# First half of the FFN's plain up tile multiplied inside the output projection stage, in accumulators that both stages share

## The chip, the core and the metric

The kernel runs on one core of one Trainium2 chip. The metric is the device time of one execution in microseconds; the kernel before has a median of 2820.73 us over three runs (2819.88 to 2821.73).

## The reference

An encoder of two layers over x (1024 tokens x 1024 features, float32). Layer 0 mixes tokens by differential attention, layer 1 by 2-D neighbourhood attention; each is followed by an output projection, a layer norm, a gated ConvFFN and another layer norm:

```python
x = layer_norm(alpha * x + mix, ln_g[i, 0], ln_b[i, 0])      # mix = heads @ w_o (+ b_o in layer 1)
ff = conv_ffn(x, ffn_w_in[i], ...)                             # h = x @ w_in + b_in; width-3 conv over tokens;
                                                               # u, g = split(h); (u * gelu(g)) @ w_out + b_out
x = layer_norm(alpha * x + ff, ln_g[i, 1], ln_b[i, 1])
```

`w_in` is 1024 x 5632: 22 tiles of 128 columns for u and 22 for g.

## The kernel before

All tensors are float32. A product is made of three matmuls in a rounded float32 form: each operand is split into a high part (a copy to the rounded form) and a low part (full minus high), and high x high, high x low and low x high are summed in PSUM.

The program is a row of stages, each with its own block of five instruction streams: attention, `output_stage` (L974), `ffn_stage` (L1155), and the same for layer 1. Between two blocks stands a barrier of all engines (`Mem.clear`, L40), and each block's buffers and PSUM are given back there. SBUF tiles X (the tokens by 128), XTh and XTl (X transposed, high and low), WH and WL (weights, eight row tiles) and `raw` (two full-precision weight slots) live across stages.

**Output stage.** Eight tiles of 128 tokens. TensorE forms `heads @ w_o` for a tile in a PSUM buffer of 1024 columns (`pg` 0 and 1 for tiles 4 to 7 in turn). VectorE adds alpha * X (`add`, L1127), in layer 1 also the bias (L1136, for tiles 4 to 7; GpSimd does it for tiles 0 to 3), takes the statistics (L913 to L917) and multiplies by the gain (L924). GpSimd takes the root of the variance (L941). Then either ScalarE scales (L948) and GpSimd shifts (L953), or, for the tiles in FINISHED (6 and 7), VectorE does both in `finish` (L932). TensorE transposes the tile (`turn`, L960, eight 128x128 transposes into `tp` 0 or 1 in turn), ScalarE makes XTh of it (`high`, L965) and VectorE XTl (`low`, L970). The turns that follow the last products (TURNS[7]) are those of tiles 5, 6 and 7; a turn waits until the low part two tiles before is done, since that frees its buffer. Both of the FFN's first two weight tiles (u tile 0 and g tile 0) are prefetched into `raw` during this stage, and at its end, behind the root of tile 7 and once all products are done, GpSimd rounds and splits them into WH[:, 6:8] and WL[:, 6:8] (L1058, L1060).

**FFN stage.** Column tile 0 (PLAIN = 1 tile) is multiplied plainly: `up_plain(a, half)` (L1408) for a = 0 (u) and 1 (g), 24 matmuls of 512 tokens for each half. The other 21 tiles go by Strassen-like sums of quarter blocks: `up_seven(f)` makes seven products M5, M2, M1, M3, M4, M7, M6 of 12 matmuls each (L1447). Their weights come in four pieces per tile (SyncE, L1286); GpSimd adds them (L1351), ScalarE makes the high part (L1614), GpSimd the low part (L1358). Their moving sides are five mixes of X: VectorE adds or subtracts token blocks (`mix_tokens`, L1794), TensorE turns them (`turn_mix`, L1423), ScalarE and VectorE split them (L1594, L1710); the fifth comes from matmuls with an identity (`sum_mix`, L1436). Small parameter vectors come as rows (L1273 to L1275) and are turned by five transposes (L1547), which wait for the three DMAs; ScalarE copies them out (L1638).

The order on TensorE before: up_plain(0, 0), the parameter transposes, turn_mix(B1), up_plain(0, 1), turn_mix(B3), up_plain(1, 0), turn_mix(B4), up_plain(1, 1), turn_mix(B7), then `up_seven(1)`: M5, M2, sum_mix(B6), M1, M3, M4, M7, M6, and `up_seven(2)`. M5 of tile 1 writes the second half of PSUM buffer 0 and M2 the first half of buffer 1, so they wait until ScalarE has taken the plain u tile (`take(0)`) and g tile (`take(1)`, L1572 and L1575). ScalarE rescales X by alpha once all four token mixes are made (L1645, L1652), before the takes. GpSimd's sum for slot i waits for product i - 4 (`made`). SyncE's queue is in order: pieces of tile 1, the bias b_out, down(0), down(1), which waits until all of X has got its bias (L1340, L1788), pieces of tile 2.

Of the kernel before, what the change touches and what calls it, by code (L numbers as in the profile page):

```python
# [20 lines left out]
P = 128  # L21
# [949 lines left out]
                                     op=ALU.subtract).then_inc(self.low_done, 1)  # L971


def output_stage(nc, name, OT, w_o, b_o, x, g, b, X, XTh, XTl, ident, alpha, raw, wh, wl, next_tiles):  # L974

# [4 lines left out]
    with ExitStack() as ctx:  # L982
# [1 line left out]
        prefetch = Prefetch(m, raw, next_tiles)  # L984
        oraw = m.sb("oraw", [P, 2, S])
        bias = m.sb("bias", [P, D])
        pg = [m.ps(f"pg{i}", [P, D]) for i in range(2)]
        tp = [m.ps(f"tp{i}", [P, KT, P]) for i in range(2)]
        FIRST = 4
        sums = [pg[0][:], pg[1][:], tp[0][:].rearrange("p k n -> p (k n)"), tp[1][:].rearrange("p k n -> p (k n)")]  # L990
# [6 lines left out]
        bias_in = m.sem("bias_in")  # L997
        first_low = m.sem("first_low")
        w_high, w_low, o_high, o_low = m.sem("w_high"), m.sem("w_low"), m.sem("o_high"), m.sem("o_low")
        product, summed, with_bias = (m.sem(s) for s in ("product", "summed", "with_bias"))  # L1000
        block = ctx.enter_context(nc.Block())

# [27 lines left out]
        @block.gpsimd  # L1030
        def _(pool):
            norm.set_power(pool)
            for k in range(1, KT):
                pool.wait_ge(w_high, k + 1)
                nc.gpsimd.tensor_tensor(out=wl[:, k], in0=raw[:, k % 2], in1=wh[:, k].bitcast(F32),
                                        op=ALU.subtract).then_inc(w_low, 1)

            def biased(t):

                pool.wait_ge(summed, t + 1)  # L1040
                nc.gpsimd.tensor_tensor(out=X[:, t], in0=X[:, t], in1=bias[:], op=ALU.add).then_inc(with_bias, 1)

            if b_o is not None:
                pool.wait_ge(bias_in, 16)
                for t in range(FIRST - 1):
                    biased(t)
            pool.wait_ge(norm.gb_in, 32)
            for t in range(TT):
                norm.root(pool, t)
                if b_o is not None and t == 0:  # L1050
                    biased(FIRST - 1)
                if t not in FINISHED:
                    norm.shift(pool, t)
            pool.wait_ge(product, TT)
            prefetch.wait(pool)
            for k in range(2):
                at = KT - 2 + k
                nc.gpsimd.tensor_scalar(wh[:, at], raw[:, k], 1.0, 1.0, ALU.mult, ALU.mult).then_inc(w_high, 1)  # L1058
                pool.wait_ge(w_high, KT + k + 1)
                nc.gpsimd.tensor_tensor(out=wl[:, at], in0=raw[:, k], in1=wh[:, at].bitcast(F32),  # L1060
                                        op=ALU.subtract).then_inc(w_low, 1)

        @block.tensor
        def _(pe):
            def products(t, k):
                for n, (o, w) in enumerate(((XTh, wh), (XTh, wl), (XTl, wh))):
                    for half in range(D // BANK):
                        last = nc.tensor.matmul(sums[t][:, half * BANK:(half + 1) * BANK],
                                                o[:, k, t * P:(t + 1) * P], w[:, k, half * BANK:(half + 1) * BANK],
                                                start=(k == 0 and n == 0), stop=(k == KT - 1 and n == 2))  # L1070
                if k == KT - 1:
                    last.then_inc(product, 1)

            for k in range(KT):
                if k == 0:
                    pe.wait_ge(first_low, 1)
                else:
                    pe.wait_ge(w_low, k)
                if k >= READY_HEADS:
                    pe.wait_ge(o_low, k - READY_HEADS + 1)  # L1080
                for t in range(FIRST):
                    products(t, k)
            for t in range(FIRST, TT):
                pe.wait_ge(summed, t - FIRST + 1 if t < FIRST + 2 else t - 1)
                for k in range(KT):
                    products(t, k)
                for u in TURNS[t]:
                    if u < 2:
                        pe.wait_ge(summed, u + 3)
                    norm.turn(pe, u)  # L1090

        @block.scalar
        def _(act):
            if b_o is not None:
                act.dma_start(bias[:], b_o.rearrange("(o d) -> o d", o=1).to_broadcast([P, D])).then_inc(bias_in, 16)
            for k in range(KT):
                if k >= 2:
                    act.wait_ge(w_in[k % 2], 16 * (k // 2))
                nc.scalar.activation(wh[:, k], raw[:, k % 2], ACT.Copy).then_inc(w_high, 1)
                if k < READY_HEADS:  # L1100
                    continue
# [12 lines left out]
        @block.vector
# [38 lines left out]


def ffn_stage(nc, name, w_in_d, b_in, conv_w, conv_b, w_out, b_out, g, b, x_out, X, XTh, XTl, ident, alpha, last_layer,  # L1155
              wraw, WH, WL, WHf, next_tiles):

# [19 lines left out]
    with ExitStack() as ctx:  # L1179
# [13 lines left out]
        prow = WDf[0:NT, 0, 0:5 * P].rearrange("p (c n) -> p c n", c=5)  # L1193
        bias = WDf[:, 1]
        gain_rows = WHf[:, 4:6]
        ph = [m.ps(f"ph{i}", [P, KT, P]) for i in range(2)]
        po = m.ps("po", [P, 4, BANK])
        flat = [ph[i][:].rearrange("p k n -> p (k n)") for i in range(2)]
        P11, P12, P21, P22 = (flat[i][:, h * BANK:(h + 1) * BANK] for i in range(2) for h in range(2))
        U = po[:, 3]  # L1200
        FINISHED = (TT - 1,)
# [197 lines left out]

        @block.tensor  # L1400
        def _(pe):
            def up_plain(a, half):
                if a and half == 0:
                    pe.wait_ge(par_set, 1)
                at = slice(half * BANK, (half + 1) * BANK)
                for k in range(KT):
                    for n, (w, x) in enumerate(((WH, XTh), (WH, XTl), (WL, XTh))):
                        last = nc.tensor.matmul(flat[a][:, at], w[:, 6 + a, k * P:(k + 1) * P], x[:, k, at],  # L1408
                                                start=(k == 0 and n == 0), stop=(k == KT - 1 and n == 2))
                if half:  # L1410
                    last.then_inc(up_done, 1)

            def turn_mix(c):

# [126 lines left out]
                            for u in range(TT - 4, TT):  # L1541
                                norm.turn(pe, u)

            up_plain(0, 0)
            pe.wait_ge(par_in, 48)
            for c in range(5):
                last = nc.tensor.transpose(flat[1][:, c * NT:(c + 1) * NT], prow[:, c], ident[0:NT, 0:NT])  # L1547
            last.then_inc(par_turned, 1)
            turn_mix(B1)
            up_plain(0, 1)  # L1550
            turn_mix(B3)
            up_plain(1, 0)
            turn_mix(B4)
            up_plain(1, 1)
            turn_mix(B7)
            for f in range(PLAIN, FT):
                up_seven(f)
# [5 lines left out]
        def _(act):  # L1563
# [71 lines left out]
            quad_copy(PLAIN, M5)  # L1635
            quad_copy(PLAIN, M2)
            act.wait_ge(par_turned, 1)
            nc.scalar.activation(par[:].rearrange("p c n -> p (c n)"), flat[1][:, 0:5 * NT], ACT.Copy).then_inc(par_set, 1)  # L1638
            mix_copy(B1)
            quad_copy(PLAIN, M1)  # L1640
            quad_copy(PLAIN, M3)
# [777 lines left out]
def build(nc, x, attn_w_qkv, attn_w_o, attn_lambda, attn_subln_g, na_w_qkv, na_b_qkv, na_rpb, na_w_o, na_b_o,  # L2419
# [10 lines left out]
    with ExitStack() as ctx:  # L2430
# [9 lines left out]
        for i in range(depth):  # L2440
            if i == 1:
                neighbourhood_stage(nc, na_w_qkv[0], na_b_qkv[0], Z, OT, XTh, XTl, ident, S, GW, KROWS, KCOLS, raw,
                                    first_rows[1])
            with ExitStack() as layer:
                X = layer.enter_context(nc.sbuf_tensor(f"X{i}", [P, S // P, D], F32))
                WH = layer.enter_context(nc.sbuf_tensor(f"WH{i}", [P, D // P, D], F32R))
                WHf = nc.alloc_sbuf_tensor_at(f"WHf{i}", [P, D // P, D], F32, offset=nc.sbuf_base - 4 * D // P * D)
                WL = layer.enter_context(nc.sbuf_tensor(f"WL{i}", [P, D // P, D], F32R))
                output_stage(nc, f"wo{i}", OT, (attn_w_o, na_w_o)[i][0], (None, na_b_o[0])[i], (x_dram, x1)[i],
                             ln_g[i, 0], ln_b[i, 0], X, XTh, XTl, ident, alpha, raw, WH, WL, first_up[i])  # L2450
                ffn_stage(nc, f"ff{i}", ffn_w_in[i], ffn_b_in[i], ffn_conv_w[i], ffn_conv_b[i], ffn_w_out[i], ffn_b_out[i],
                          ln_g[i, 1], ln_b[i, 1], (x1, out_dram)[i], X, XTh, XTl, ident, alpha, i == depth - 1, raw, WH,
                          WL, WHf, first_qk)


_INS = ["x", "attn_w_qkv", "attn_w_o", "attn_lambda", "attn_subln_g", "na_w_qkv", "na_b_qkv", "na_rpb", "na_w_o",
# [18 lines left out]
```

## Time and profile before

| | us |
|---|---|
| median of 3 runs | 2820.73 |
| the profiled execution | 2821.15 |
| its span | 2819.2 |
| TensorE busy in the span | 2661.5 (94%) |
| VectorE busy | 1937.4 (69%) |
| GpSimd busy | 1675.8 (59%) |
| ScalarE busy | 1183.6 (42%) |

The mean granted TensorE clock is 0.976 of full speed. Layer 0's output stage ends and its FFN stage begins at 773 us of the span, layer 1's at 2122.8 us. In the profile PE is TensorE, DVE VectorE, ACT ScalarE, POOL GpSimd, SP SyncE. Matmuls overlap, so a group's busy time is longer than the distance of their starts. A row of a timeline has the start and the length in us, the engine, the line, the operation, output and inputs, the count, and in brackets the engine's idle time before it with what ended it. A row of the chain has start, length and count. A row of busy time has the stretch, its length, the busy us of PE, its weight loads, DVE, ACT and POOL, the granted TensorE clock (1.00 is 2.4 GHz, its other level is 1.2), the DMA share and GB/s.

### The profile page before, as it was taken

Reading aid. Unit: us, or ns where it says so; the run is one execution under the profiler, and the core shown is the slowest. Engines: PE = TensorE matmul, PEld = TensorE weight load, DVE = VectorE, ACT = ScalarE, POOL = GpSimd, SP = SyncE. Lnnn points to the kernel's source line nnn. Section 1 sums busy time; section 2 is a strip of 40 time slices with the busy share of each in tenths; the row PEclk is TensorE's granted clock in tenths of the full one; section 3 lists DMA queues with packets and bytes.
Section 4 is the critical chain, followed back from the end, with each engine's and each line's share of the span. In section 5 each row is a group of like instructions: output and inputs, shape, how many; then the busy total and the mean of one; then the engine's idle time right before and its main releaser. Section 6 shows DMA issues by size and latency. Waiting matters only on the chain. (4 is left out here: it accounts for less than half of the span.)

```text
span 2819.2 us, 35798 instructions
## 1 busy us (share of the span) xinstructions
PE 2661.5 (94%) x13043; PEld 2224.7 (79%) x13043; DVE 1937.4 (69%) x2476; ACT 1183.6 (42%) x1762; POOL 1675.8 (59%) x1179
## 2 busy tenths in 40 slices
PE   7999999988899999999989999998798999999997
PEld 6888888776778888888867888887677888888886
DVE  3666676683677766677783777777567777666778
ACT  3455445553253333333333555555415333333332
POOL 2434443334487767777754666664457776677776
PEclk9999999998999999999999999999899999999999
DMA  3010000235021112121221221212411111121212
GB/s 116 26 30 30 28 22 30 61 96 176 11 65 48 45 57 64 46 60 46 65 85 44 60 59 45 52 44 53 134 61 54 58 47 45 60 60 45 60 45 90
DMA packets 214043, 163.82 MB, mean 58 GB/s; under 512 B 36283, under 2 KB 195595, under 8 KB 213899
## 3 DMA queue, kind: packets, MB, share of 16 engines
q1 hardware_dynamic: 213755, 161.38, 19.4%
q8 instruction: 89, 1.46, 0.2%
q14 instruction: 55, 0.45, 0.1%
q10 hardware_dynamic: 144, 0.52, 0.1%
HBM read 137.24 MB, written 24.64 MB: 57 GB/s over the span
## 5 line engine op out<-in xcount | busy, mean ns | idle before, releaser
L1351 POOL TENSOR_TENSOR ff_Rlf<-raw_weights 128x512 f32<-128x512 f32 x210 | 330.8, 1588 | 53.4 <-PE ff_ph L1447 33.1
L1358 POOL TENSOR_TENSOR ff_Rl<-ff_Rlf,ff_Rh 128x512 fp32r<-128x512 f32 x210 | 310.8, 1497 | 25.1 <-ACT ff_Rh L1614 25.1
L1358 POOL TENSOR_TENSOR ff_Rl<-raw_weights,ff_Rh 128x512 fp32r<-128x512 f32 x84 | 157.9, 1889 | 253.5 <-ACT ff_Rh L1614 253.5
L1614 ACT ACTIVATE ff_Rh<-ff_Rlf 128x512 fp32r<-128x512 f32 x210 | 130.5, 630 | 364.1 <-POOL ff_Rlf L1351 363.8
L1447 PE MATMUL ff_ph<-XTh,ff_Rh 128*128 128x512 f32 x672 | 263.0, 391 | 8.1 <-POOL ff_Rl L1358 7.8
L1447 PE MATMUL ff_ph<-XTl,ff_Rh 128*128 128x512 f32 x672 | 262.3, 390 | 0.0
L1447 PE MATMUL ff_ph<-XTh,ff_Rl 128*128 128x512 f32 x672 | 262.3, 390 | 0.0
L1494 PE MATMUL ff_po<-ff_WDh,WH 128*128 128x512 f32 x624 | 244.6, 392 | 1.8 <-DVE X L1861 1.8
L1494 PE MATMUL ff_po<-ff_WDh,WL 128*128 128x512 f32 x624 | 242.9, 389 | 0.0
L1494 PE MATMUL ff_po<-ff_WDl,WH 128*128 128x512 f32 x624 | 242.9, 389 | 0.0
L1717 DVE TENSOR_TENSOR X<-ff_po,X 128x512 f32<-128x512 f32 x288 | 191.3, 683 | 66.0 <-PE ff_po L1494 66.0
L2058 POOL TENSOR_SCALAR na_E<-na_E,na_rden 128x512 f32<-128x512 f32 x128 | 104.6, 818 | 194.0 <-DVE na_rden L2405 193.3
L687 ACT ACTIVATE da_E<-da_S,da_mn 128x1024 f32<-128x1024 f32 x112 | 125.1, 1117 | 198.0 <-DVE da_mn L782 197.8
L1725 DVE SCALAR_TENSOR_TENSOR ff_C<-ff_H,ff_par,ff_C 128x1024 f32<-128x1024 f32 x88 | 161.8, 1838 | 53.9 <-ACT ff_C L1631 52.5
L1447 PE MATMUL ff_ph<-WH,ff_Rl 128*128 128x512 f32 x504 | 196.1, 389 | 0.0
L1447 PE MATMUL ff_ph<-WL,ff_Rh 128*128 128x512 f32 x504 | 196.1, 389 | 0.0
L1447 PE MATMUL ff_ph<-WH,ff_Rh 128*128 128x512 f32 x504 | 196.1, 389 | 0.0
L324 POOL TENSOR_SCALAR da_E<-da_E,da_rden,da_neglam 128x1024 f32<-128x1024 f32 x64 | 76.6, 1197 | 198.5 <-DVE da_rden L790 198.5
L1731 DVE SCALAR_TENSOR_TENSOR ff_C<-ff_H,ff_par,ff_C 128x1024 f32<-128x1024 f32 x88 | 166.1, 1887 | 1.0
L782 DVE CUSTOM_DVE_ANT_0 da_S<-da_S,da_strip 128x1024 f32<-128x1024 f32 x128 | 154.0, 1241 | 12.1 <-PE da_S L418 11.8
L404 PE MATMUL da_pa<-XTh,da_wh 128*128 128x512 f32 x360 | 151.0, 419 | 10.0 <-POOL da_wl L318 3.8
L1447 PEld LDWEIGHTS ff_ph<-XTh,ff_Rh 128*128 128x128 f32 x672 | 126.5, 188 | 38.1 <-issue 10.8
(319 smaller groups left out, 7466.5 us busy)
## 6 DMA issues: line engine op xcount, KB each, us to landing
raw_weights<-in_ffn_w_in SPq DMA_DIRECT2D x168, 256.0 KB, 3.4
ff_WDlf<-in_ffn_w_out SPq DMA_DIRECT2D x40, 512.0 KB, 4.3
raw_weights<-in_attn_w_qkv SPq DMA_DIRECT2D x24, 512.0 KB, 3.7
raw_weights<-in_na_w_qkv SPq DMA_DIRECT2D x24, 512.0 KB, 4.2
rpb_rows<-da_rows SPq DMA_DIRECT2D x2, 3840.0 KB, 26.8
na_B<-rpb_rows SPq DMA_DIRECT2D x32, 224.0 KB, 4.5
wo_oraw<-heads_t SPq DMA_DIRECT2D x12, 512.0 KB, 4.6
da_E<-in_x SPq DMA_DIRECT2D x8, 512.0 KB, 6.2
```

The lines of the kernel that those rows point to most:

```text
L404: last = nc.tensor.matmul(out[:], w[:, j // 2, k], x[:, k, t0:t0 + BANK], start=(i == 0), stop=(i == 3 * KT - 1))
L687: nc.scalar.activation(E[:, t % 2, c], Sc[c][:], ACT.Exp, scale=-1.0, bias=mn[:, t % 2, c:c + 1], accum_out=den[:, t % 2, c:c + 1]).then_i ...
L782: nc.vector.tensor_tensor_reduce(out=Sc[c][:], in0=Sc[c][:], in1=strip[:, (QT - 1 - t) * P:(QT - 1 - t) * P + S], scale=1.0, scalar=3.0e38 ...
L1351: nc.gpsimd.tensor_tensor(out=Rf[:, i % SLOTS], in0=quad(*a), in1=quad(*b), op=op).then_inc(quad_sum, 1)
L1358: nc.gpsimd.tensor_tensor(out=Rl[:, i % SLOTS], in0=src, in1=Rh[:, i % SLOTS].bitcast(F32), op=ALU.subtract).then_inc(quad_low, 1)
L1447: last = nc.tensor.matmul(out, w, x[:, k], start=(k == 0 and n == 0), stop=(k == HK - 1 and n == 2))
L1494: last = nc.tensor.matmul(out, a[:, t * P:(t + 1) * P], w[:, half * BANK:(half + 1) * BANK], start=(f == first and j == 0), stop=(f == las ...
L1614: nc.scalar.activation(Rh[:, i % SLOTS], src, ACT.Copy).then_inc(quad_high, 1)
L1717: nc.vector.tensor_tensor(out=at, in0=po[:, r % 4], in1=at, op=ALU.add).then_inc(added, 1)
L1725: nc.vector.scalar_tensor_tensor(out=C[:, parity], in0=H[:, parity, 0:S], scalar=par[:, 1, idx:idx + 1], in1=C[:, parity], op0=ALU.mult, o ...
L1731: nc.vector.scalar_tensor_tensor(out=C[:, parity], in0=H[:, parity, 2:S + 2], scalar=par[:, 3, idx:idx + 1], in1=C[:, parity], op0=ALU.mul ...
L2058: nc.gpsimd.tensor_scalar(E[:, b], E[:, b], rden[:, b:b + 1], 1.0, ALU.mult, ALU.mult).then_inc(scaled, 1)
```

## The change

In both layers the two PSUM buffers of 1024 columns are allocated outside the stages (`acc`), and serve as `pg` in the output stage and as `ph` in the FFN stage. The first half (tokens 0 to 511) of both plain up tiles is multiplied in the output stage, `up_half(0)` between the turns of tiles 6 and 7, `up_half(1)` behind the turn of tile 7. For that, GpSimd rounds and splits the prefetched weights into buffers of their own (`up_high`, `up_low`) behind the root of tile 6, and not behind that of tile 7; WH[:, 6:8] and WL[:, 6:8] are still in use by the last products then. ScalarE copies the high part to WH and GpSimd the low part to WL when all products are done. In the FFN stage `up_plain` does the second half alone, and the five parameter transposes use the other half of their buffer.

```diff
@@ output_stage
+        up_high, up_low = m.sb("up_high", [P, 2, D], F32R), m.sb("up_low", [P, 2, D], F32R)
-        pg = [m.ps(f"pg{i}", [P, D]) for i in range(2)]
+        pg = acc
...
@@ output_stage, gpsimd
+            def split_up():
+                prefetch.wait(pool)
+                for k in range(2):
+                    nc.gpsimd.tensor_scalar(up_high[:, k], raw[:, k], 1.0, 1.0, ALU.mult, ALU.mult).then_inc(up_rounded, 1)
+                    pool.wait_ge(up_rounded, k + 1)
+                    nc.gpsimd.tensor_tensor(out=up_low[:, k], in0=raw[:, k], in1=up_high[:, k].bitcast(F32),
+                                            op=ALU.subtract).then_inc(up_split, 1)
...
                 if t not in FINISHED:
                     norm.shift(pool, t)
+                if t == TT - 2:
+                    split_up()
             pool.wait_ge(product, TT)
-            prefetch.wait(pool)
+            pool.wait_ge(up_split, 2)
             for k in range(2):
-                at = KT - 2 + k
-                nc.gpsimd.tensor_scalar(wh[:, at], raw[:, k], 1.0, 1.0, ALU.mult, ALU.mult).then_inc(w_high, 1)
-                pool.wait_ge(w_high, KT + k + 1)
-                nc.gpsimd.tensor_tensor(out=wl[:, at], in0=raw[:, k], in1=wh[:, at].bitcast(F32),
-                                        op=ALU.subtract).then_inc(w_low, 1)
+                nc.gpsimd.tensor_scalar(wl[:, KT - 2 + k], up_low[:, k].bitcast(F32), 1.0, 1.0, ALU.mult,
+                                        ALU.mult).then_inc(up_copied, 1)
@@ output_stage, tensor
+            def up_half(a):
+                pe.wait_ge(up_split, a + 1)
+                pe.wait_ge(summed, TT - 1 + a)
+                for k in range(KT):
+                    for n, (w, x) in enumerate(((up_high, XTh), (up_high, XTl), (up_low, XTh))):
+                        nc.tensor.matmul(acc[a][:, 0:BANK], w[:, a, k * P:(k + 1) * P], x[:, k, 0:BANK],
+                                         start=(k == 0 and n == 0), stop=(k == KT - 1 and n == 2))
...
                     if u < 2:
                         pe.wait_ge(summed, u + 3)
+                    if u == TT - 1:
+                        pe.wait_ge(norm.low_done, TT // 2)
+                        up_half(0)
                     norm.turn(pe, u)
+            up_half(1)
@@ output_stage, scalar
                 for u in TURNS[t]:
+                    if u == TT - 1:
+                        act.wait_ge(product, TT)
+                        act.wait_ge(up_rounded, 2)
+                        for k in range(2):
+                            nc.scalar.activation(wh[:, KT - 2 + k], up_high[:, k].bitcast(F32), ACT.Copy).then_inc(up_copied, 1)
                     norm.high(act, u)
@@ ffn_stage
-        ph = [m.ps(f"ph{i}", [P, KT, P]) for i in range(2)]
+        ph = [a[:].rearrange("p (k n) -> p k n", n=P) for a in acc]
@@ ffn_stage, tensor
-            def up_plain(a, half):
-                if a and half == 0:
+            def up_plain(a):
+                at = slice(BANK, 2 * BANK)
+                if a:
                     pe.wait_ge(par_set, 1)
-                at = slice(half * BANK, (half + 1) * BANK)
...
-                if half:
-                    last.then_inc(up_done, 1)
+                last.then_inc(up_done, 1)
...
-            up_plain(0, 0)
             pe.wait_ge(par_in, 48)
             for c in range(5):
-                last = nc.tensor.transpose(flat[1][:, c * NT:(c + 1) * NT], prow[:, c], ident[0:NT, 0:NT])
+                last = nc.tensor.transpose(flat[1][:, BANK + c * NT:BANK + (c + 1) * NT], prow[:, c], ident[0:NT, 0:NT])
             last.then_inc(par_turned, 1)
             turn_mix(B1)
-            up_plain(0, 1)
+            up_plain(0)
             turn_mix(B3)
-            up_plain(1, 0)
+            up_plain(1)
             turn_mix(B4)
-            up_plain(1, 1)
             turn_mix(B7)
@@ build
+                acc = [layer.enter_context(nc.psum_tensor(f"acc{i}_{j}", [P, D], F32)) for j in range(2)]
```

## Rows read from the trace of the kernel before

**Rows 1.** Waits of TensorE, layer 0's FFN stage: total us, times, longest us.

```profile
PE ff_ph L1447 <- POOL ff_Rl L1358: 3.1, 1, 3.1
```

**Rows 2.** Timeline, layer 0's FFN head: start us, us, engine, line, tiles [idle before].

```profile
780.69 2.52 POOL L1351 TENSOR_TENSOR ff_Rlf<-raw_weights 128x512 f32<-128x512 f32 x2 [7.58 <-DMA raw_weights<-in_ffn_w_in]
...
783.24 0.63 ACT L1614 ACTIVATE ff_Rh<-ff_Rlf 128x512 fp32r<-128x512 f32 x1 [0.61 <-POOL ff_Rlf L1351]
...
793.71 3.90 ACT L1645 ACTIVATE X<-X 128x1024 f32<-128x1024 f32 x4 [2.65 <-DVE ff_WDhf L1794]
...
798.56 2.36 DVE L1710 TENSOR_TENSOR WL<-ff_po,WH 128x1024 fp32r<-128x1024 f32 x2 [2.08 <-ACT WH L1594]
...
806.21 1.22 ACT L1575 ACTIVATE ff_C<-ff_ph,ff_centre,ff_par 128x1024 f32<-128x1024 f32 x1
...
807.48 0.50 PE L1447 MATMUL ff_ph<-XTh,ff_Rh 128*128 128x512 f32 x1
...
816.59 3.53 POOL L1351 TENSOR_TENSOR ff_Rlf<-raw_weights 128x512 f32<-128x512 f32 x2
...
830.88 0.56 PE L1447 MATMUL ff_ph<-XTh,ff_Rh 128*128 128x512 f32 x1 [3.11 <-POOL ff_Rl L1358]
...
838.05 0.39 PE L1447 MATMUL ff_ph<-WH,ff_Rh 128*128 128x512 f32 x1
```

**Rows 3.** Timeline, ScalarE, head of layer 1's FFN stage.

```profile
2147.02 1.94 ACT L1594 ACTIVATE WH<-ff_po 128x1024 fp32r<-128x1024 f32 x2 [0.85 <-PE ff_po L1423]
```

**Rows 4.** Timeline, TensorE, from layer 0's output stage into the FFN stage.

```profile
759.51 1.91 PE L960 MATMUL wo_tp<-ident,X 128*128 128x128 f32 x16
...
767.66 1.94 PE L960 MATMUL wo_tp<-ident,X 128*128 128x128 f32 x8 [6.24 <-DVE XTl L970]
...
773.02 0.76 PE L1408 MATMUL ff_ph<-XTh,WH 128*128 128x512 f32 x1 [3.42 <-PEq L43]
```

**Rows 5.** Timeline, GpSimd and VectorE, end of layer 0's output stage.

```profile
764.26 1.04 POOL L1058 TENSOR_SCALAR WH<-raw_weights 128x1024 fp32r<-128x1024 f32 x1
...
764.38 1.99 DVE L932 SCALAR_TENSOR_TENSOR X<-X,wo_rstd,wo_gb 128x1024 f32<-128x1024 f32 x1 [0.51 <-POOL wo_rstd L941]
...
765.39 3.20 POOL L1060 TENSOR_TENSOR WL<-raw_weights,WH 128x1024 fp32r<-128x1024 f32 x1
...
769.69 2.35 POOL L1060 TENSOR_TENSOR WL<-raw_weights,WH 128x1024 fp32r<-128x1024 f32 x1
```

**Rows 6.** Chain that ended last, up halves of layer 1.

```profile
2122.78 8.26 PE ff_ph L1408 x24
...
2133.38 5.50 PE ff_ph L1408 x24
```

**Rows 7.** Timeline, TensorE, start of the kernel.

```profile
4.51 3.65 PE L552 MATMUL da_S<-ident,da_E 128*128 128x128 f32 x16 [4.51 <-DMA da_E<-in_x]
...
8.92 1.07 PE L552 MATMUL da_S<-ident,da_E 128*128 128x128 f32 x8 [0.76 <-DVE XTl L719]
...
34.18 0.50 PE L404 MATMUL da_pa<-XTh,da_wh 128*128 128x512 f32 x1 [2.63 <-DVE XTl L719]
```

**Rows 8.** Timeline, GpSimd and VectorE, layer 0's FFN stage at 811.

```profile
811.00 3.41 POOL L1365 TENSOR_TENSOR ff_WDl<-ff_WDlf,ff_WDh 128x1024 fp32r<-128x1024 f32 x1
...
812.05 5.66 DVE L1788 TENSOR_TENSOR X<-X,ff_WDlf 128x1024 f32<-128x1024 f32 x2
```

**Rows 9.** Timeline, end of layer 1's output stage.

```profile
2102.25 1.55 POOL L941 TENSOR_TENSOR wo_rstd<-wo_ve,wo_power 128x1 f32<-128x1 f32 x1
...
2108.02 1.91 PE L960 MATMUL wo_tp<-ident,X 128*128 128x128 f32 x16
...
2109.47 1.22 DVE L1136 TENSOR_TENSOR X<-X,wo_bias 128x1024 f32<-128x1024 f32 x1
...
2117.43 1.94 PE L960 MATMUL wo_tp<-ident,X 128*128 128x128 f32 x8 [7.50 <-DVE XTl L970]
```

**Rows 10.** Busy time of each engine by stretch, layer 0's first up half.

```profile
773.00:780.30 7.30, 7.28 (x24) 5.61 (x24) 4.49 (x2) 1.57 (x2) 0.11 (x2) 0.76 0.54 161
```

More of the change, by code:

```diff
@@ L971, in low, with output_stage @@
                                      op=ALU.subtract).then_inc(self.low_done, 1)
-def output_stage(nc, name, OT, w_o, b_o, x, g, b, X, XTh, XTl, ident, alpha, raw, wh, wl, next_tiles):
+def output_stage(nc, name, OT, w_o, b_o, x, g, b, X, XTh, XTl, ident, alpha, raw, wh, wl, next_tiles, acc):
     S, D = x.shape
@@ L999, in output_stage @@
         w_high, w_low, o_high, o_low = m.sem("w_high"), m.sem("w_low"), m.sem("o_high"), m.sem("o_low")
+        up_rounded, up_split, up_copied = m.sem("up_rounded"), m.sem("up_split"), m.sem("up_copied")
         product, summed, with_bias = (m.sem(s) for s in ("product", "summed", "with_bias"))
@@ L1155, in ffn_stage @@
 def ffn_stage(nc, name, w_in_d, b_in, conv_w, conv_b, w_out, b_out, g, b, x_out, X, XTh, XTl, ident, alpha, last_layer,
-              wraw, WH, WL, WHf, next_tiles):
+              wraw, WH, WL, WHf, next_tiles, acc):
     D = w_in_d.shape[0]
@@ L1195, in ffn_stage @@
         gain_rows = WHf[:, 4:6]
-        ph = [m.ps(f"ph{i}", [P, KT, P]) for i in range(2)]
+        ph = [a[:].rearrange("p (k n) -> p k n", n=P) for a in acc]
         po = m.ps("po", [P, 4, BANK])
-        flat = [ph[i][:].rearrange("p k n -> p (k n)") for i in range(2)]
+        flat = [a[:] for a in acc]
         P11, P12, P21, P22 = (flat[i][:, h * BANK:(h + 1) * BANK] for i in range(2) for h in range(2))
@@ L1637, in _ @@
             act.wait_ge(par_turned, 1)
-            nc.scalar.activation(par[:].rearrange("p c n -> p (c n)"), flat[1][:, 0:5 * NT], ACT.Copy).then_inc(par_set, 1)
+            nc.scalar.activation(par[:].rearrange("p c n -> p (c n)"), flat[1][:, BANK:BANK + 5 * NT], ACT.Copy).then_inc(par_set, 1)
             mix_copy(B1)
@@ L2448, in build @@
                 WL = layer.enter_context(nc.sbuf_tensor(f"WL{i}", [P, D // P, D], F32R))
+                acc = [layer.enter_context(nc.psum_tensor(f"acc{i}_{j}", [P, D], F32)) for j in range(2)]
                 output_stage(nc, f"wo{i}", OT, (attn_w_o, na_w_o)[i][0], (None, na_b_o[0])[i], (x_dram, x1)[i],
-                             ln_g[i, 0], ln_b[i, 0], X, XTh, XTl, ident, alpha, raw, WH, WL, first_up[i])
+                             ln_g[i, 0], ln_b[i, 0], X, XTh, XTl, ident, alpha, raw, WH, WL, first_up[i], acc)
                 ffn_stage(nc, f"ff{i}", ffn_w_in[i], ffn_b_in[i], ffn_conv_w[i], ffn_conv_b[i], ffn_w_out[i], ffn_b_out[i],
                           ln_g[i, 1], ln_b[i, 1], (x1, out_dram)[i], X, XTh, XTl, ident, alpha, i == depth - 1, raw, WH,
-                          WL, WHf, first_qk)
+                          WL, WHf, first_qk, acc)
 _INS = ["x", "attn_w_qkv", "attn_w_o", "attn_lambda", "attn_subln_g", "na_w_qkv", "na_b_qkv", "na_rpb", "na_w_o",
```

## The prediction

> **What bounds the kernel now.** I read the page's busy line first (TensorE 94% of the span), then who TensorE waits for in each FFN stage, then the timelines of all engines around the two changes of stage, since this edit touches only those. In layer 0's FFN stage TensorE's only long idle time besides the change of stage is 3.1 us [rows 1]. It stands at the second tile's first product, at 830.88 [rows 2]; behind it TensorE runs without a gap to the layer's end. So what counts is when that product starts, in both layers.
>
> What sets that start is in the rows between 773 and 831 [rows 2]. GpSimd forms its first weight sum at 780.69, when the pieces land that were asked for at the stage's start (7.6 us of idle). ScalarE's copy of the second sum (783.24) waits for GpSimd. The token mixes, VectorE's, follow, and at 793.71 ScalarE starts rescaling X right behind a wait for the last mix on VectorE. From there ScalarE has copies and biases without a gap to 806.21 + 1.22 = 807.43, and product M2 starts at 807.48, since it overwrites what that last ScalarE instruction (`take(1)`) reads. None of these waits names TensorE. TensorE's plain up halves lie beside this chain, and the chain hangs on the start of the stage (T0), because the weight pieces are asked for there. In layer 1 the two run level: one ScalarE copy at 2147.02 waited 0.85 us for TensorE [rows 3]. So removing up-matmuls behind T0 is worth nothing in layer 0 and at most 0.85 us in layer 1, and whatever moves T0 later is lost in full.
>
> **The end of the output stage, layer 0.** Today: TensorE turns tokens tiles 5 and 6 (759.51 + 1.91 = 761.42), idles 6.24 us, turns tile 7 at 767.66, and the FFN's first matmul is at 773.02 [rows 4]. The last to end is GpSimd's second low part, 769.69 + 2.35 = 772.04 [rows 5], so the barrier costs 0.98 us.
> After: the first up half (24 matmuls) goes into the 6.24 us. At the full clock 24 of them take 5.50 us, at the slow one, partly, 8.26 [rows 6]. TensorE comes to it from dense work, so 5.50: 761.42 to 766.9. It needs only tiles 0 to 3 and GpSimd's first split, done at about 757; free. The turn of tile 7 starts at 767.66 as before, because its release (VectorE, behind its layer norm of tile 7) doesn't move. It then takes 1.07 us and not 1.94: after an idle time of 0.76 us eight transposes took 1.07 [rows 7]. That is 768.7. Now the second half follows, 5.50, to 774.2, and TensorE is last into the barrier where GpSimd was. T0 = 774.2 + 0.98 = 775.2: **2.2 us later**. GpSimd's work there shrinks (two 1.04 us copies instead of 1.04 + 3.20 + 1.04 + 2.35), and ScalarE's two new copies fall into its own idle time: nothing. The DMA queue of SyncE has nothing moved past it before T0.
>
> **The end of the output stage, layer 1.** Here the split, moved ahead of the root of tile 7, meets a bias add that layer 0 doesn't have. Two instructions that each read two SBUF operands exclude one another on VectorE and GpSimd: two VectorE adds (1.22 each alone) took 5.66 us while GpSimd's subtraction (811.00, 3.41) and the next one ran [rows 8]; the first waited until 814.41. The same shows in rows 5: VectorE's 764.38 took 1.99, until GpSimd's 764.26 was through, and GpSimd's 765.39 took 3.20 against 2.35 alone. Now place the split: GpSimd's root of tile 6 ends at 2102.25 + 1.55 = 2103.80 [rows 9]. From there the same pattern as from 764.26 in layer 0 (rounding at 0, subtraction at +1.13 held up by VectorE's norm of tile 6, rounding at +4.30, subtraction at 769.69 - 764.26 = +5.43) puts the second subtraction at 2109.23 to 2111.58. VectorE's bias add of tile 7 wants to start at 2109.47, 0.24 us too late: it waits until 2111.58, **2.1 us**. Behind it on VectorE stand statistics, gain, finish and the low parts that free the buffer for the turn of tile 7; they all shift, and the turn starts at 2117.43 + 2.1 = 2119.5. The bounds of this wait are 0.7 (VectorE comes first, and only its gain waits) and 2.4 (a whole subtraction).
> TensorE: tiles 5 and 6 end at 2108.02 + 1.91 = 2109.93, first half to 2115.4, idle 4.1 us. After 2.63 us of idle a matmul still ran at the full clock [rows 7], after 3.11 us not: the 24 matmuls from 830.88 to 838.05 took 7.17 us, not 5.50 [rows 2]. So the turn is at the slow clock, 1.94, to 2121.45. At the kernel's start transposes alone ran slow for 3.65 us, and eight that followed were at the full clock [rows 7]; 1.7 us of slow matmuls remain, which costs half of it, 0.8. Second half: 2121.45 + 5.50 + 0.8 = 2127.75, + 0.98 = 2128.7, against 2122.78 [rows 6]: **5.9 us later**. (Bounds: turn and half at the full clock, 4.2; a half of 8.26, 7.9; without the bias wait and warm, 2.2.)
> Rows 7 bear on a rule of the Trainium skill, "TensorE: Matmul & The Clock Gate", Part 4: PE-mode transpose, by which transposes do not bring the full clock. The trace speaks against it. By the page, the second half would take 8.26 in layer 1, 2.0 us more than my 6.3.
>
> **Inside the FFN stage.** Of TensorE's work 24 matmuls of 7.28 us (granted clock 0.76 [rows 10]; 8.26 in layer 1) and 24 of 5.50 are gone. The parameter columns are then turned as soon as their DMAs land, some 4 us behind T0, where TensorE starts slow, but the first ScalarE copy that needs the first mix comes at T0 + 11 anyhow. From T0 to M2 nothing gets shorter in layer 0. M5 now starts when the last mix can be turned, behind VectorE's split of the one before it (798.56 + 2.36, T0 + 27.9 [rows 2]), at about T0 + 28.8, is through at 31.6 and M2 still has to wait for `take(1)` at T0 + 34.4. That is 2.8 us of idle, between the 2.63 that kept the clock and the 3.11 that lost it; with TensorE thinly used ahead of it I take it as lost. M2 and what follows come 1.7 to 2.8 us later (7.17 or 8.26 against 5.50), take 2.0. Most is free, as TensorE idled 3.1 us ahead of 830.88. GpSimd's sum for M6 waits for M1's end: it started at 816.59 + 1.77 = 818.36, some 1.6 behind M1, so it loses 0.4, and so do the next pieces and M5 of the next tile. But the idle time ahead of that M5 shrinks to 1.5 us, and its slow start (7.17 - 5.50 = 1.7) goes. Layer 0: 0.4 - 1.7 = **-1.3**. In layer 1 the 24 matmuls there ran at the full clock already; the late M1 costs **+0.4** and eats the 0.85. (If the clock holds through the 2.8 us: 0 in layer 0, -0.85 to +0.85 in layer 1.) The down-projection weight, asked for 2 us earlier behind T0, is the one DMA that moves; ScalarE takes it at T0 + 36: nothing. The bank that the five parameter transposes use is another one, at no cost.
>
> **Sum.** 2.2 + 5.9 - 1.3 + 0.4 = 7.2 us. The profiled execution took 2821.15 us (span 2819.2, so 2 us around it), 0.4 above the median 2820.73: 2821.15 + 7.2 - 0.4 = 2828.0, 0.26% slower.
>
> **Rivals.**
> No hold-up in layer 1: the split wins or loses the race by more than I think, or GpSimd runs a little later, and the turn stays at a full clock: T0 + 2.2 to 2.9 in both layers, with -1.3 to 0.4 behind: 3 to 5 us, 2825. For it: a margin of 0.24 us only. Against: the distances in rows 5 are of the same four instructions in the same order.
> TensorE is the bound of the FFN's head after all, and the other engines move up with it: then what counts is 7.28 + 5.50 - 2.2 = 10.6 us in layer 0 and 8.26 + 5.50 - 5.9 = 7.9 in layer 1: 2802. The wait of 0.85 us in layer 1 speaks for it, the waits of GpSimd and ScalarE in rows 2 against it. It decides if M2 starts earlier than T0 + 34; half of it would give 2812.
> The slow clock bites harder: transposes don't raise it, so the second half in layer 1 costs 8.26 (+2.0), and up halves and mixes behind T0 are late enough (1.8 to 2.8) to hold ScalarE's copy at T0 + 24 up by about 1 in each layer: +4, 2832.
>
> **Chances.** Forecast 0.53, no hold-up 0.28, TensorE bound 0.10, clock 0.09. About 0.2% (5.6 us) is what a measurement can tell from no change; 2826.4 is that bound. So slower 0.62, the same 0.28, faster 0.10. The range leaves out most of the TensorE case and takes in the others: 2820 to 2832.5.
>
> **What would show it.** The FFN's first DMA 2 us later against the stage before it in layer 0 and about 6 in layer 1; the bias add of tile 7 in layer 1 lasting about 3.3 us; the turn of tile 7 1.07 us long in layer 0 and 1.94 in layer 1; M2 at T0 + 34 in both layers with some 3 us of idle ahead of it; no slow start at the second tile in layer 0. I am wrong if M2 comes at T0 + 31 or earlier, or if TensorE isn't the last into the barrier.

## The result, and the profile after

The changed kernel takes 2829.26 us (median of 7 runs, 2827.89 to 2831.06) against 2820.73 before: ratio 1.0029, 95% interval 1.0019 to 1.0039. It is slower, by 8.5 us. The profiled execution's span is 2827.3 us against 2819.2.

Both stages' ends are read against the same event, VectorE's add of token tile 7 (start at 759.71 in layer 0 and 2108.22 in layer 1 before), since whatever ran earlier shifts all later rows by some tenths. T0 is SyncE's first DMA of the FFN stage. The last column pair is the start of M5 of tile 2 behind T0, the first product from which TensorE runs without a gap, but for two waits of 1.8 and 1.2 us in layer 1 that both kernels have.

| kernel | T0 behind the add, layer 0 / 1 | M5 of tile 2 behind T0, layer 0 / 1 |
|---|---|---|
| before | 13.27 / 14.52 | 57.90 / 57.45 |
| changed | 15.39 / 20.08 | 57.09 / 57.85 |

So T0 is 2.12 us later in layer 0 and 5.56 in layer 1, and behind T0 nothing was got back but 0.8 us in layer 0. The end of the output stage in layer 0, TensorE's and GpSimd's timelines (the second half's first and last matmul, the turn, GpSimd's copies that were the last work before):

```profile
761.70 0.47 PE L1090 MATMUL acc<-XTh,wo_up_high 128*128 128x512 f32 x1
...
768.20 1.06 PE L960 MATMUL wo_tp<-ident,X 128*128 128x128 f32 x8 [0.77 <-DVE XTl L970]
769.01 0.48 PE L1090 MATMUL acc<-XTh,wo_up_high 128*128 128x512 f32 x1
...
774.34 0.39 PE L1090 MATMUL acc<-XTh,wo_up_low 128*128 128x512 f32 x1
778.28 0.51 PE L1573 MATMUL acc<-ident,ff_WDlf 44*128 44x44 f32 x5 [3.55 <-DMA ff_WDlf<-in_ffn_conv_b]
```

```profile
764.79 3.03 POOL L1070 TENSOR_SCALAR WL<-wo_up_low 128x1024 fp32r<-128x1024 f32 x2
775.63 0.10 POOL L1360 MEMSET ff_H<- 128x2 f32 x1 [7.81 <-POOLq L43]
```

Against [rows 4], the first half fills the idle time of 6.24 us down to 0.77, and the turn of tile 7 takes 1.06 and not 1.94. But then TensorE is busy until 774.73, and GpSimd, the last before ([rows 5]), idles 7.81 us at the barrier. Before, GpSimd was last by 0.12 us only: VectorE's low part of tile 7, which hangs on the turn, ended at 771.92:

```profile
770.69 1.23 DVE L970 TENSOR_TENSOR XTl<-wo_tp,XTh 128x1024 fp32r<-128x1024 f32 x1 [2.05 <-ACT XTh L965]
```

The end of the output stage in layer 1, GpSimd's, VectorE's and TensorE's timelines:

```profile
2106.19 3.26 POOL L1051 TENSOR_TENSOR wo_up_low<-raw_weights,wo_up_high 128x1024 fp32r<-128x1024 f32 x1
2109.42 1.06 POOL L1049 TENSOR_SCALAR wo_up_high<-raw_weights 128x1024 fp32r<-128x1024 f32 x1
2110.56 2.40 POOL L1051 TENSOR_TENSOR wo_up_low<-raw_weights,wo_up_high 128x1024 fp32r<-128x1024 f32 x1
```

```profile
2109.51 1.22 DVE L1155 SCALAR_TENSOR_TENSOR X<-X,acc 128x1024 f32<-128x1024 f32 x1
2110.77 3.27 DVE L1164 TENSOR_TENSOR X<-X,wo_bias 128x1024 f32<-128x1024 f32 x1
```

```profile
2120.77 1.94 PE L960 MATMUL wo_tp<-ident,X 128*128 128x128 f32 x8 [4.06 <-DVE XTl L970]
2122.36 0.78 PE L1090 MATMUL acc<-XTh,wo_up_high 128*128 128x512 f32 x1
2122.93 0.63 PE L1090 MATMUL acc<-XTl,wo_up_high 128*128 128x512 f32 x1
...
2128.30 0.39 PE L1090 MATMUL acc<-XTh,wo_up_low 128*128 128x512 f32 x1
```

The bias add asked at 2110.77, 0.21 us behind the start of GpSimd's second subtraction at 2110.56, and ended 1.08 us behind that one's end (2112.96): it took 3.27 us and not 1.22 ([rows 9]). Behind T0, the waits of TensorE in layer 0 (engine line, what it waited for, total us, times, longest us):

```profile
PE ff_po L1450 <- DVE WL L1735: 4.3, 3, 2.3
PE acc L1573 <- DMA ff_WDlf<-in_ffn_conv_b: 3.5, 1, 3.5
PE acc L1474 <- POOL ff_Rl L1386: 3.1, 1, 3.1
PE acc L1474 <- ACT ff_C L1600: 1.1, 1, 1.1
```

That is where the matmuls that left the FFN stage went: TensorE, whose one such wait before was that for GpSimd ([rows 1]), now also idles for the parameter rows, for the splits of the mixes, and at M2 for `take(1)`. And the layer 0 rows that answer to [rows 2], each set against T0 (775.63):

```profile
782.62 2.54 POOL L1379 TENSOR_TENSOR ff_Rlf<-raw_weights 128x512 f32<-128x512 f32 x2 [6.84 <-DMA raw_weights<-in_ffn_w_in]
...
795.61 3.91 ACT L1670 ACTIVATE X<-X 128x1024 f32<-128x1024 f32 x4 [4.03 <-DVE ff_WDhf L1819]
...
801.83 3.01 PE L1450 MATMUL ff_po<-ident,ff_WDhf 128*128 128x128 f32 x16 [2.30 <-DVE WL L1735]
...
809.37 0.50 PE L1474 MATMUL acc<-XTh,ff_Rh 128*128 128x512 f32 x1 [1.12 <-ACT ff_C L1600]
832.72 0.47 PE L1474 MATMUL acc<-XTh,ff_Rh 128*128 128x512 f32 x1 [3.06 <-POOL ff_Rl L1386]
```

The chain is the old one: pieces land at T0 + 7.0 (7.7 before), the rescale starts at + 20.0 (20.7), M2 at + 33.7 (34.5). It starts 0.7 us earlier because the pieces landed 0.7 us earlier; all behind it in layer 0 follows. Layer 1 is told further down.

### The profile page after: what moved, and what is told of

Read it like the earlier page. It is cut to its first block and busy times, and to the rows that moved or that the text cites. A ratio compares the mean times of both kernels' runs of the same rounds, so it can differ in the third digit from the quotient of the medians.

```text
span 2827.3 us, 35812 instructions
## 1 busy us (share of the span) xinstructions
PE 2666.5 (94%) x13043; PEld 2228.4 (79%) x13043; DVE 1938.8 (69%) x2476; ACT 1187.0 (42%) x1766; POOL 1679.8 (59%) x1183
## 5 line engine op out<-in xcount | busy, mean ns | idle before, releaser
L1474 PE MATMUL acc<-XTh,ff_Rh 128*128 128x512 f32 x672 | 264.8, 394 | 11.0 <-POOL ff_Rl L1386 8.6
L1474 PE MATMUL acc<-XTl,ff_Rh 128*128 128x512 f32 x672 | 263.6, 392 | 0.0
L1474 PE MATMUL acc<-XTh,ff_Rl 128*128 128x512 f32 x672 | 263.4, 392 | 0.0
L1474 PE MATMUL acc<-WH,ff_Rl 128*128 128x512 f32 x504 | 196.1, 389 | 0.0
L1474 PE MATMUL acc<-WL,ff_Rh 128*128 128x512 f32 x504 | 196.1, 389 | 0.0
L1474 PE MATMUL acc<-WH,ff_Rh 128*128 128x512 f32 x504 | 196.1, 389 | 0.0
L1474 PEld LDWEIGHTS acc<-XTh,ff_Rh 128*128 128x128 f32 x672 | 127.5, 190 | 41.4 <-issue 11.1
```

The lines of the kernel that those rows point to most:

```text
L1474: last = nc.tensor.matmul(out, w, x[:, k], start=(k == 0 and n == 0), stop=(k == HK - 1 and n == 2))
```

## The experiments

In all of them the times are medians of 7 to 10 runs, next to runs of the kernel before on the same chip (2819.34 to 2821.21 us); the ratio is to those. Places behind T0 are of one profiled execution each. e3 leaves part of the computation out, the others none.

**e1, the split earlier.**

```diff
                if t not in FINISHED:
                    norm.shift(pool, t)
-                if t == TT - 2:
-                    split_up()
+                if t in (3, 4):
+                    split_up(t - 3)
```

> The changed kernel with GpSimd's split of the up weights earlier: one tile behind the shift of tile 3, the other behind that of tile 4, and not both behind the root of tile 6. My theory (in layer 1 the split holds up VectorE's bias add of tile 7 by 2.1 us, and the end of the stage with it): that add is 1.22 us long again and not 3.27, the turn of tile 7 in layer 1 starts about 2.1 us earlier against the add of tile 7, the idle time before it is 2.0 us and not 4.1, so it is at the full clock (1.07, not 1.94), and T0 of layer 1 comes about 3.4 us earlier; layer 0 stays as in the changed kernel. Time about 2825.5. Rival (the hold-up is hidden behind the second half, or something else made layer 1 late): within 1 us of the changed kernel, 2829.

Measured: 2826.05 us, ratio 1.0016 (1.0007 to 1.0026), where the change has 1.0029. T0 behind the add is 15.42 and 18.23: 1.85 us back in layer 1, not 3.4. VectorE's and TensorE's timelines in layer 1:

```profile
2114.10 1.23 DVE L1165 TENSOR_TENSOR X<-X,wo_bias 128x1024 f32<-128x1024 f32 x1
```

```profile
2122.05 1.06 PE L960 MATMUL wo_tp<-ident,X 128*128 128x128 f32 x8 [2.06 <-DVE XTl L970]
2122.87 0.48 PE L1091 MATMUL acc<-XTh,wo_up_high 128*128 128x512 f32 x1
2123.19 0.49 PE L1091 MATMUL acc<-XTl,wo_up_high 128*128 128x512 f32 x1
2123.48 0.63 PE L1091 MATMUL acc<-XTh,wo_up_low 128*128 128x512 f32 x1
```

The bias add is 1.23 us long, and the turn comes 9.20 us behind the add (before 9.21, changed 11.26). So the hold-up is shown, with its 2.06 us. The turn at the full clock gave 0.8 us more, but the clock fell a few matmuls into the second half, and the 24 took 7.1 us (2122.87 to 2130.0), where they had taken 6.2 in the changed kernel and I had expected 5.5. What is left of the gain is 1.85.

**e2, only the u tile's half moved.**

```diff
-            up_half(1)
...
-            up_plain(1)
+            up_plain(1, 0)
             turn_mix(B4)
+            up_plain(1, 1)
```

> The changed kernel with only the u tile's first half in the output stage; the g tile's is back in the FFN stage. My theory (the second half is what makes T0 late, and work behind T0 is free): TensorE's last work before the barrier is the turn of tile 7 at the full clock, T0 of layer 0 is 0.9 us EARLIER than in the kernel before against the add of tile 7, layer 1's is 2.1 us later than before (the bias add's wait), though 24 matmuls more are behind T0 than in the change. Time 2821 to 2823. Rival (TensorE's work behind T0 counts): the 5.5 us of matmuls that are back cost as much as the earlier T0 gives, 2829.

Measured: 2819.34 us, ratio 0.9997 (0.9987 to 1.0006). T0 is at 12.27, a full 1.0 us earlier than before, and 16.44, 1.92 later (the bias add is 3.27 us long again). M5 of tile 2 stands at T0 + 57.23 and 57.39: with 24 matmuls more behind T0 than in the change it is 0.14 us later in layer 0 and 0.46 earlier in layer 1. About 9 us of difference to the change is thus T0's 3.1 + 3.6 us and 1.1 of clock (the 84 matmuls from that M5 to the first of the down-projection took 19.64 us in layer 0 and not 20.77); the rival falls.

**e3, the up halves nearly taken out of the kernel before.**

```diff
+                steps = KT if half else 1
-                for k in range(KT):
+                for k in range(steps):
```

> The kernel before with the first halves of both plain up tiles cut to 3 of 24 matmuls each (7 of 8 feature blocks are left out of tokens 0 to 511 of the plain tile), nothing added anywhere. It takes away 42 matmuls per layer behind T0, some 11 us of TensorE. My theory (the head of the FFN hangs on the weight pieces asked for at T0): M2 of tile 1 stays at T0 + 34, and the time falls by 0 to 1.5 us, to about 2820; it may rise by 1 to 2 if the slow clock at the second tile gets longer. Rival (TensorE bounds the head): 8 to 10 us less in each layer, about 2802.

Measured: 2819.73 us beside 2821.21, ratio 0.9993 (0.9984 to 1.0003): no change that can be told. 84 matmuls, 19 us at the full clock, left out for nothing. Where M2 comes was not as expected: T0 + 36.67 and 35.83, not 34, and M5 of tile 2 is 0.77 and 0.89 us later than before. TensorE's timeline in layer 0 shows what it did instead: it idled before the parameter rows and before the third mix, and the transposes that followed ran at the slow clock:

```profile
774.49 0.76 PE L1548 MATMUL ff_ph<-ident,ff_WDlf 44*128 44x44 f32 x5 [2.33 <-DMA ff_WDlf<-in_ffn_conv_b]
...
793.21 3.65 PE L1424 MATMUL ff_po<-ident,ff_C 128*128 128x128 f32 x16 [5.48 <-DVE WL L1711]
```

**e4, both edits.** The split as in e1, the halves as in e2.

> Both of the first two edits: early split, and only the u tile's first half in the output stage. My theory: T0 is 0.9 us earlier than in the kernel before in both layers, nothing else moves; against that stands up to 1.3 us in layer 1 if the slow clock at the second tile comes as in the changed kernel. 2819 to 2820.5, the same as or slightly faster than the kernel before. Rival (the moved work pays behind T0 too): 7 us less in each layer than before, 2806.

Measured: 2818.13 us, ratio 0.9990 (0.9980 to 0.9999). T0 is at 12.25 and 13.51, 1.02 and 1.01 us earlier than before; M5 of tile 2 at + 57.32 and + 57.00. Against e7 below, which has the early split and no half moved (T0 at 13.13 and 14.37), T0 is 0.88 and 0.86 us earlier. This is what the first half is worth where it is put: the turn of tile 7 at the full clock. The early split, with e7's early pieces, is the other 0.14.

**e5, e6, e7, the pieces of tile 1 asked for in the output stage.** All three have the early split; e5 has the first half alone, e6 both, e7 none. `first_pieces` is the full weight tile 1, and SyncE asks for its four pieces in the order of the FFN stage, which then asks for them no more (last line of the cut).

```diff
+            sp.wait_ge(up_split, 2)
+            for gate, k in ((0, 1), (1, 1), (0, 0), (1, 0)):
+                src = first_pieces[gate][:, k * KT // 2:(k + 1) * KT // 2]
+                sp.dma_start(raw[:, gate, k * BANK:(k + 1) * BANK].rearrange("p (k n) -> p k n", k=KT // 2),
+                             src).then_inc(pieces_in, 16)
+            sp.wait_ge(pieces_in, 64)
...
-            pieces(PLAIN)
```

> The early split with only the u tile's first half moved (as in the run before), and in addition the weight pieces of tile 1 are asked for in the output stage, as soon as the up weights are split, not at T0. My theory (behind T0 the chain starts with the landing of those pieces, some 7 us, and TensorE's work lies beside it): GpSimd's first sum starts at T0 + 0.1 and not + 7; ScalarE's first mix copy waits for TensorE's turn and comes at T0 + 5 instead of + 11; now TensorE bounds the head: M2 at T0 + 32, M5 of tile 2 at T0 + 52 without an idle time before it, against + 57 to 58. With T0 1 us earlier than before that is about 15 us in all, 2806. Rival (the pieces are not the head of the chain; the parameter rows or the mixes are): M5 of tile 2 stays at T0 + 56 or later, 2817.

> Early split, both first halves in the output stage, and the pieces of tile 1 asked for there too. My theory: T0 is as late as in the run with the early split alone (2.1 and 3.7 us later than before), behind it M2 waits for ScalarE again at T0 + 28, and M5 of tile 2 comes at T0 + 52, where GpSimd's chain sets it. 2815, so the second half in the output stage still loses against the first alone. Rival (with the pieces there TensorE is the only bound, and every matmul moved ahead of T0 pays): the same as or faster than with the first half alone, 2806 or less.

> Early split and early pieces, but no half moved: both up halves stay in the FFN stage as in the kernel before. My theory: TensorE is busy without a gap from T0 to M5 of tile 2, which comes at T0 + 55 with no idle time and no slow start: 2814. So moving the first half is worth about 8 us once the pieces are early, while it is worth 2 without. Rival (the pieces alone carry the gain): equal to the run with pieces and first half, within 2 us.

Measured: e5 2811.96 us, ratio 0.9970 (0.9959 to 0.9981); e6 2820.54, 0.9998 (0.9989 to 1.0008); e7 2818.01, 0.9991 (0.9981 to 1.0000). The pieces are the head of the chain: in e5 M5 of tile 2 comes at T0 + 54.61 and 54.87. It is half of the 5 us that I expected. GpSimd's, VectorE's and ScalarE's timelines in e5's layer 0 (T0 at 772.81) show the next link:

```profile
772.92 6.64 POOL L1386 TENSOR_TENSOR ff_Rlf<-raw_weights 128x512 f32<-128x512 f32 x2
```

```profile
775.07 3.36 DVE L1829 TENSOR_TENSOR ff_H<-X 128x2048 f32<-128x2048 f32 x1
```

```profile
776.31 0.63 ACT L1649 ACTIVATE ff_Rh<-ff_Rlf 128x512 fp32r<-128x512 f32 x1 [1.88 <-POOL ff_Rlf L1386]
779.59 0.63 ACT L1649 ACTIVATE ff_Rh<-ff_Rlf 128x512 fp32r<-128x512 f32 x1 [2.64 <-POOL ff_Rlf L1386]
```

Two sums that took 2.52 us ([rows 2]) take 6.64, since VectorE's two token mixes of X, with two SBUF operands each, start at T0 as well, and ScalarE waits for the second. The second half still loses: e6 is 8.6 us slower than e5, and T0 (15.40 and 18.24 against 12.25 and 14.38) is 7.0 of them; M5 of tile 2 comes at + 54.12 and 54.88, not at the 52 that I expected. In e7 the parameter turn stands behind 24 up-matmuls, 14 and 8 of them at the slow clock, and comes at T0 + 8.5 and 7.2. TensorE is then busy up to M2, as expected, but M5 of tile 2 is at + 57.68 and 56.36, not 55. So the early pieces without the first half gave 2.5 us, the first half without the early pieces 3.1 (e4), and both 8.5: with the pieces early TensorE's work behind T0 does count. All three have the early split, which was not run alone.

**e8, ScalarE's order behind T0, without the early pieces.** Early split, first half alone.

```diff
-            quad_copy(PLAIN, M5)
-            quad_copy(PLAIN, M2)
             act.wait_ge(par_turned, 1)
...
             mix_copy(B1)
+            quad_copy(PLAIN, M5)
+            quad_copy(PLAIN, M2)
```

> Early split and the u tile's first half alone in the output stage, pieces asked for at T0 as in the kernel before; ScalarE's order behind T0 is changed: the copy of the parameters and of the first mix stand ahead of the copies of the first two weight sums, for which it waits until the pieces land. My theory (the chain runs pieces, first sums, ScalarE, mix copy, token mixes, rescale, M2): the rescale starts at about T0 + 15 instead of + 21, M2 at T0 + 32 is set by TensorE, GpSimd's low parts (to T0 + 18) then start its bias adds, and M5 of tile 2 comes at T0 + 54.5 instead of + 57.2. About 3 us per layer less than with the same kernel in the old order: 2812. Rival (the order on ScalarE doesn't matter, only when the pieces land): 2818, M5 of tile 2 at T0 + 57.

Measured: 2814.67 us, ratio 0.9983 (0.9973 to 0.9992). M5 of tile 2 at T0 + 56.24 and 56.49, 1.1 and 0.5 us earlier than in e4, where I expected 2.7. The direction is as expected, the size is not, and the interval overlaps that of e4 (0.9980 to 0.9999), so against the rival speaks only the trace. The rescale starts at T0 + 19.0, not 15, because ScalarE now waits 5.95 us for GpSimd's third sum, which VectorE's mixes hold up:

```profile
788.20 0.63 ACT L1641 ACTIVATE ff_Rh<-ff_Rlf 128x512 fp32r<-128x512 f32 x1 [5.95 <-POOL ff_Rlf L1379]
```

**e9, both.** As e5, with the copies of the parameters and of the first mix ahead of the second sum's copy.

> As the run before and with the pieces of tile 1 asked for in the output stage; ScalarE's order is sum M5, parameters, first mix, sum M2. In the earlier run with early pieces GpSimd's first two sums took 6.6 us, held up by VectorE's two token mixes, and ScalarE waited for the second. My theory: taken off that wait, the rescale starts at T0 + 15 and not + 17, M5 of tile 2 comes at T0 + 52 where TensorE alone sets it, with no idle time before it: 2807. Rival (GpSimd stays behind VectorE and sets M5 of tile 2 whatever ScalarE does): 2812 as with the early pieces in the old order.

Measured: 2819.5 us, ratio 1.0001 (0.9992 to 1.0011): 7.5 us slower than e5. My theory for this run is wrong. The rescale did start at T0 + 15.0 in layer 0; VectorE's and GpSimd's timelines show what that set free, and VectorE's in the kernel before what the last two had taken there:

```profile
785.62 1.29 DVE L1837 TENSOR_TENSOR ff_centre<-ff_par 128x44 f32<-128x44 f32 x1
786.95 1.22 DVE L1839 TENSOR_TENSOR ff_centre<-ff_centre,ff_par 128x44 f32<-128x44 f32 x1
788.09 4.72 DVE L1841 TENSOR_TENSOR ff_delta<-ff_par 128x22 f32<-128x22 f32 x2
```

```profile
788.07 9.33 POOL L1374 TENSOR_TENSOR X<-X,ff_WDlf 128x1024 f32<-128x1024 f32 x4
```

```profile
793.95 0.27 DVE L1806 TENSOR_TENSOR ff_delta<-ff_par 128x22 f32<-128x22 f32 x2
```

GpSimd's bias adds (2.3 us each) follow the rescale. Of four VectorE instructions on 44 and 22 columns, 0.19, 0.21 and for the last two together 0.27 us in the kernel before, the first two wait for a low part of GpSimd's and the last two for a bias add each. The split of the second mix is queued behind them, and M5 of tile 2 comes at + 58.46 and 61.52.

**e10, those four moved ahead.**

```diff
             mix_tokens(B3)
+            dve.wait_ge(par_set, 1)
+            ...                            # centre (2), delta (2)
             mix_lower(B1)
```

> As the run before (early split, first half alone, early pieces, ScalarE's mix copy ahead of the second sum), and VectorE's four tiny instructions on the parameters (128x44 and 128x22, two SBUF operands each) stand ahead of its split of the first mix instead of behind the last token mix. There they took 7.2 us in layer 0, between and behind GpSimd's bias adds. My theory (the earlier rescale lets GpSimd's bias adds loose on them, and they hold the split of the second mix, TensorE's turn of the third and M2): they take under 1 us, TensorE's idle time before the third turn falls from 3.6 us to under 1, M2 comes at T0 + 32 and M5 of tile 2 at T0 + 53 to 54: 2809. Rival (the bias adds hold up other VectorE instructions just the same): 2816 to 2820.

Measured: 2814.6 us, ratio 0.9980 (0.9970 to 0.9990). Most of the loss of e9 is back (M5 of tile 2 at + 55.44 and 54.51), but not all of what was expected: at their new place the four take 5.06 us in layer 0 beside GpSimd's sums and low parts, and ScalarE's rescale is at T0 + 17.4. The mix copy moved ahead has gained nothing over e5 in either run. Of all ten, e5 is the fastest, 8.5 us below the kernel before and 17 below the change.

## Why the prediction was right

**T0 in layer 0.** Forecast 2.2 us later, measured 2.12. The steps hold one by one: the first half free, the turn of 1.06 us, TensorE last into the barrier, which costs 0.90 behind TensorE's modelled end. e2 and e4 show the cause: without the second half T0 is 1.0 us early, 3.1 us earlier than with it.

**T0 in layer 1.** Forecast 5.9, measured 5.56. The hold-up of 2.1 us was 2.05, and e1 and e4 take it away with the overlap. The turn at the slow clock was 1.94 as said. The second half lost 0.6 us by the clock, not 0.8: it had three slow matmuls. Its 6.2 us are far from the 8.26 of the rival by which transposes don't raise the clock.

**The head hangs on the pieces, not on TensorE.** e3 shows it from one side (42 matmuls less per layer, nothing gained), e5 from the other. The rival that TensorE is the bound is out for this change; it would have made e3 8 to 10 us faster per layer. e7 shows where it comes back: once the pieces are early.

**Inside the FFN stage** the sum was wrong in its working. Forecast -1.3 in layer 0 and +0.4 in layer 1. Measured -0.81 and, with the clock, +1.52. I had M5 of tile 1 at the full clock, then 2.8 us idle, then a slow M2. In fact the clock fell one step earlier: the turn of the last mix took 3.01 us, M5 started slow, the wait for `take(1)` shrank to 1.1 us and M2 ran at the full clock. So M1 wasn't late, the 0.4 us through GpSimd's sum for M6 didn't come, and the idle time ahead of M5 of tile 2 stayed at 3.06 us with its slow start, so the 1.7 us weren't saved. What moved that M5 by -0.81 was the landing of the pieces, T0 + 6.99 after 7.71. SyncE's four requests for them had taken longer before:

```profile
774.15 2.87 SPq L1286 DMA_DIRECT2D raw_weights<-in_ffn_w_in  x4
```

```profile
776.82 2.04 SPq L1314 DMA_DIRECT2D raw_weights<-in_ffn_w_in  x4
```

In layer 1 the forecast's +0.4 agrees with a measured +0.40 by luck, for it came by another path. The first sum started at + 6.89 after 6.28 and the second at + 8.83 after 7.79, and the rescale with them 1.05 us later. Its second half started only 0.07 later, since ScalarE no longer waits 0.85 us for TensorE's third turn ([rows 3]); what is left of the lateness are GpSimd's and the next pieces' steps, which no run takes apart. The idle time ahead of that M5 grew from 2.36 to 3.19 us, the clock fell there, and the 84 matmuls up to the down-projection took 20.77 us after 19.65 (start of M5 to start of the first of the down-projection): 1.12 us that I had excluded. Why the landings differ stays open. The earlier request for the down-projection weight, at T0 + 4, isn't enough for it: e3 has it too, at T0 + 5.1 and 4.1, and has first sums at T0 + 7.95 and 6.45, near those of the kernel before, while e2, e4 and e8 have them at + 6.8 to 7.2 in both layers.

Sum of what was measured: 2.12 + 5.56 - 0.81 + 0.40 + 1.12 = 8.4 us. The two profiled spans differ by 8.1 us: up to the add of layer 0 there are 0.5 more, between M5 of tile 2 and layer 1's add 0.5 less, and behind the 84 matmuls of layer 1 0.3 less. The medians differ by 8.53. The time came right because the two T0 terms were: forecast 8.1, measured 7.7. The terms inside the FFN stage, forecast -0.9, came to +0.7.

## What to carry to other kernels

Work moved across a barrier pays only if it fits into idle time ahead of the barrier: the first half did, the second made TensorE last and moved T0 by 3.2 us in layer 0 and 4.7 in layer 1 (e4 to e1), while behind the barrier it had been hidden. Ask which transfer a stage asks for first: the time from the barrier to its landing, some 7 us here, hid the matmuls that were moved. Asking for it earlier gave 2.5 us, moving the first half 3.1, and both 8.5. Before moving a GpSimd instruction, lay it against VectorE's instructions with two SBUF operands, not only against who waits for it; in [rows 5] a GpSimd instruction with one SBUF operand (764.26) held VectorE's (764.38) up too.

## What the runs showed of the hardware

- VectorE and GpSimd exclude one another instruction by instruction also when one of them is tiny: a VectorE instruction of 128x22 elements waited 2.3 us for each GpSimd add of 128x1024 (e9), 0.27 us for two of them otherwise.
- The length of an idle time doesn't tell whether TensorE's clock falls. Behind 2.05 us the turn of tile 7 took 1.07 us in e4's layer 1, behind 2.04 us 1.94 in e5's. Ahead of M5 of tile 2, the clock stayed up behind 3.30 us in e2's layer 0, and fell behind 2.36 us in e7's layer 1; behind 2.36 us in e7's layer 0 it stayed up. So the forecast's step from 2.63 us (kept, [rows 7]) to 3.11 (lost, [rows 2]) was no bound, and the 1.12 us of clock in layer 1 needn't be in every execution. The two stretches, in e2 and e7, with the granted clock third from the end:

```profile
827.99:835.00 7.01, 7.01 (x31) 5.80 (x32) 4.09 (x4) 5.02 (x7) 7.01 (x5) 1.00 0.00 0
```

```profile
2177.71:2185.00 7.29, 7.29 (x25) 5.86 (x26) 4.38 (x4) 4.42 (x6) 7.29 (x5) 0.77 0.00 1
```

- The clock can fall under load. In e1, behind 2.06 us of idle, eight transposes ran in 1.06 us, and the clock fell during the matmuls behind them: 0.50 was granted from 2123.5 to 2126.5, with TensorE busy throughout.
- Transposes alone brought the clock back in one place: in the changed kernel's layer 0 the FFN stage's first 21, from 778.28, ran slow (granted clock 0.57), and the up-matmuls from 781.98 at the full clock after the first. In layer 1 the same 21 ran mostly at the full clock (0.82) and the matmuls behind them slow (0.53). At the kernel's start, on which the prediction rests ([rows 7]), the transposes' durations speak of a slow clock, but the granted clock of 4.50 to 8.16 us reads 1.00.

```profile
778.28:781.98 3.70, 3.70 (x22) 3.65 (x22) 1.89 (x1) 0.00 (x0) 0.00 (x0) 0.57 0.92 270
```

```profile
2132.22:2134.85 2.63, 2.63 (x22) 2.58 (x22) 1.90 (x1) 0.00 (x0) 0.00 (x0) 0.82 0.92 272
2134.85:2137.50 2.65, 2.65 (x9) 2.13 (x8) 0.00 (x0) 0.00 (x0) 1.02 (x1) 0.53 0.86 281
```
